# Decoder layer on one core: reordering in out, up and down, and four sums per chunk on VectorE

## What is computed

```python
mix = hybrid_mixer(x, w_in, b_gates, w_sc_conv, mh_gain, w_out)   # gated convolution | mLSTM, then w_out
x = layer_norm(alpha * x + mix, ln1_g, ln1_b)
hid = causal_dwconv(einsum('bsd,df->bsf', x, w_up), w_ffn_conv, b_ffn_conv)
val, gate = hid[..., :5632], hid[..., 5632:]
ff = einsum('bsf,fd->bsd', silu(gate) * val, w_down)
x = layer_norm(alpha * x + ff, ln2_g, ln2_b)
```

## Time and profile before

| | |
|---|---|
| median of 3 runs | 2234.39 us (2232.96 to 2235.47) |
| profiled execution | 2231.34 us, of it span 2229.5 us |
| granted TensorE clock, mean | 0.987 |
| busy in the span | PE 2152.3, PEld 1926.9, DVE 1550.8, ACT 937.4, POOL 233.1 us |
| chain that ended last | PE 82%, DVE 8%, DMA 5%, issue 3%, ACT 2% |

### The profile page before, as it was taken

How to read it: one execution, slowest core, us unless ns; L and a number is a source line. 1 busy time by engine, 2 the same in 40 slices (tenths; PEclk the granted TensorE clock), 3 DMA queues, 4 the chain that set the end, 5 groups by cost and what they waited for, 6 DMA issues and landing times.

```text
span 2229.5 us, 31156 instructions
## 1 busy us (share of the span) xinstructions
PE 2152.3 (97%) x12984; PEld 1926.9 (86%) x12984; DVE 1550.8 (70%) x1612; ACT 937.4 (42%) x1092; POOL 233.1 (10%) x197
## 2 busy tenths in 40 slices
PE   8999999999999998899999999999999999999994
PEld 7888888888877878899999999999999878888873
DVE  3354324432339997777777777777777799999998
ACT  4332222221124445455555455554555544444441
POOL 0000000000011212000000000000000123221220
PEclk9999999999999999999999999999999999999997
DMA  6222222242238414667666766676666788775451
GB/s 233 94 95 87 84 94 82 89 170 94 94 136 212 124 76 142 188 171 190 185 176 169 209 182 168 184 200 170 161 175 180 255 201 233 208 232 149 142 177 76
DMA packets 86249, 350.46 MB, mean 157 GB/s; under 512 B 8172, under 2 KB 19468, under 8 KB 73056
## 3 DMA queue, kind: packets, MB, share of 16 engines
q1 hardware_dynamic: 63616, 263.22, 33.9%
q0 software_dynamic: 22496, 85.30, 19.5%
HBM read 324.36 MB, written 24.12 MB: 156 GB/s over the span
## 4 chain that ended last, share of the span: by engine, by line
PE 82%; DVE 8%; DMA 5%; issue 3%; ACT 2%; SPq 0%; POOL 0%; DVEq 0%; ACTq 0%; POOLq 0%
PE ps L1686 27%; PE ps L1687 27%; PE ps L1688 27%; DMA unit_odd<-w_up 2%; DVE slot_lo L1410 1%; DMA hb<-h_dram 1%; DVE acc L1616 1%; ACT slot_hi L924 1%; DMA oa<-w_out 1%; DVE oslot_lo L1282 1%; DVE slot_lo L1564 1%; DMA raw<-w_mix 1%; DMA unit_even<-w_up 0%; DVE acc L1636 0%; DVE dx L1588 0%
## 5 line engine op out<-in xcount | busy, mean ns | idle before, releaser
L1686 PE MATMUL ps<-xb,slot_hi 128*128 128x256 f32 x2408 | 687.1, 285 | 17.5 <-DVE hid L1432 10.0
L1687 PE MATMUL ps<-xb,slot_hi 128*128 128x256 f32 x2408 | 683.5, 284 | 0.0
L1688 PE MATMUL ps<-xb,slot_lo 128*128 128x256 f32 x2408 | 683.2, 284 | 0.0
L1686 PEld LDWEIGHTS ps<-xb,slot_hi 128*128 128x128 f32 x2408 | 463.9, 193 | 24.4 <-DVE slot_lo L1410 16.4
L1688 PEld LDWEIGHTS ps<-xb,slot_lo 128*128 128x128 f32 x2408 | 464.1, 193 | 0.0
L1687 PEld LDWEIGHTS ps<-xb,slot_hi 128*128 128x128 f32 x2408 | 464.1, 193 | 0.0
L722 ACT ACTIVATE w_hi<-raw 128x2048 fp32r<-128x2048 f32 x56 | 107.3, 1916 | 424.6 <-PE ps L1688 422.0
L1073 DVE TENSOR_TENSOR w_lo<-raw,w_hi 128x2048 fp32r<-128x2048 f32 x55 | 125.8, 2288 | 213.7 <-ACT w_hi L722 213.7
L1410 DVE TENSOR_TENSOR slot_lo<-unit_odd,slot_hi 128x1024 fp32r<-128x1024 f32 x154 | 188.7, 1225 | 99.3 <-ACT slot_hi L924 99.0
L1410 DVE TENSOR_TENSOR slot_lo<-unit_even,slot_hi 128x1024 fp32r<-128x1024 f32 x147 | 180.0, 1224 | 105.8 <-ACT slot_hi L924 105.6
L1686 PE MATMUL ps<-act_hi,w_hi 128*128 128x512 f32 x640 | 249.7, 390 | 0.0
(11 more groups left out here) (224 smaller groups left out, 3585.2 us busy)
## 6 DMA issues: line engine op xcount, KB each, us to landing
raw<-w_mix SPq DMA_DIRECT2D x56, 1024.0 KB, 4.7
unit_odd<-w_up SPq DMA_DIRECT2D x88, 512.0 KB, 6.2
unit_even<-w_up SPq DMA_DIRECT2D x84, 512.0 KB, 6.4
da<-w_down SPq DMA_DIRECT2D x16, 2048.0 KB, 11.4
unit_odd<-w_up POOLq DMA_DIRECT2D x44, 512.0 KB, 9.9
unit_even<-w_up POOLq DMA_DIRECT2D x42, 512.0 KB, 9.9
da<-w_down POOLq DMA_DIRECT2D x20, 1024.0 KB, 9.9
oa<-w_out SPq DMA_DIRECT2D x6, 2048.0 KB, 9.8
```

Source lines behind the costliest of these rows:

```text
L1686: pe.matmul(dst, a[0], b[0], start=first, stop=False, skip_group_check=onto)
L1687: pe.matmul(dst, a[0], b[1], start=False, stop=False, skip_group_check=onto)
L1688: return pe.matmul(dst, a[1], b[0], start=False, stop=last, skip_group_check=onto)
```

## The change

Four things, three of order and one of engine:

1. out: POOL issues the s1 accumulates before the sums; in chunk 0 the sums also wait for four out_lo. SP waits for both s1 accumulates before it loads A12 (and A22 behind it).
2. up, group 1: DVE's `hid_add` stands ahead of `up_lo_part`; SP stores hidden tile 0 after the loads of group 3's weights, not before.
3. down, start: SP loads A12 of chunk 0 after hb21 and the store of hidden tile GROUPS - 1.
4. down: t1 to t4 of each chunk move from POOL to DVE, at fixed slots. POOL keeps the DMAs; in chunk 1 its residual accumulate stands ahead of s3. The semaphores yc_hi and hc_hi become one (tokens_hi), counted on.

```diff
@@ SP, out
             load_out(0, A21, oa21)
+            for i in range(2):
+                sp.wait_ge(s1_added[i], 16)
             load_out(0, A12, oa12)
@@ SP, up
             for m in range(1, GROUPS - 1):
-                store_hidden(m - 1)
+                if m > 1:
+                    store_hidden(m - 1)
                 for b, i in FREED:
...
                     load_unit_block(m + 2, b)
+                if m == 1:
+                    store_hidden(0)
@@ SP, start of down
             load_hidden(0, 3, hb22)
-            sp.wait_ge(up_done, N_UP - NP + 2)
-            load_block(0, A12, da12)
             sp.wait_ge(up_lo, N_UP - NP + 3)
             sp.wait_ge(s4_up, GROUPS)
             load_hidden(0, 2, hb21)
             store_hidden(GROUPS - 1)
+            sp.wait_ge(up_done, N_UP - NP + 2)
+            load_block(0, A12, da12)
@@ POOL, out
-            pool.wait_ge(ym_h, 8)
-            pool.wait_ge(conv_u, 8)
             for c in range(OUT_CHUNKS):
                 y11, y12, y21, y22 = out_blocks(c)
+                for p in (0, 2):
+                    out_s1(c, p)
                 if c:
-                    for p in (0, 2):
-                        out_s1(c, p)
                     pool.wait_ge(yc_lo, NP * c)
+                else:
+                    pool.wait_ge(ym_h, 8)
+                    pool.wait_ge(conv_u, 8)
+                    pool.wait_ge(out_lo, 4)
                 pool.tensor_tensor(ty[:, :, :], y12, y11, ALU.subtract).then_inc(t1_sum, 1)
-                if c == 0:
-                    for p in (0, 2):
-                        out_s1(c, p)
@@ POOL, down (down_t1 to down_t4 removed)
             for c in range(CHUNKS):
                 g = CHUNK_PAIRS[c]
-                down_t1(c, g)
-                down_t2(c, g)
+                if c == 1:
+                    add_residual(0, 1, NP)
                 for p in range(0, g, 2):
                     down_s3(c, p)
-                down_t3(c, g)
-                if c == 1:
-                    add_residual(0, 1, NP)
-                down_t4(c, g)
@@ DVE, up
                 m, i = unit_of(n)
+                add = n and ORDER[(n - 1) % NP] in ("P2", "P7", "P3")
+                if add and m == 1:
+                    hid_add(n - 1)
                 if n + AHEAD < N_UP:
                     up_lo_part(n + AHEAD)
...
-                if n and ORDER[(n - 1) % NP] in ("P2", "P7", "P3"):
+                if add and m > 1:
                     hid_add(n - 1)
@@ DVE, down
+            def down_t4(c):
+                g = CHUNK_PAIRS[c]
+                dve.wait_ge(hb_in[2], 16 * (c + 1))
+                dve.wait_ge(t2_sum, OUT_CHUNKS + c + 1)
+                dve.wait_ge(hc_lo, NP * c + 4)
+                dve.tensor_tensor(hy[:, 0:g, :], hb21[:, 0:g, :], hb11[:, 0:g, :], ALU.subtract).then_inc(t4_sum, 1)
...
                 if s + DOWN_AHEAD < N_DOWN:
                     down_lo_part(s + DOWN_AHEAD)
+                if s == 0:
+                    down_t1(0)
+                if s == 1:
+                    down_t2(0)
+                if i == 6 and c + 1 < CHUNKS and p in (1, 2):
+                    (down_t1 if p == 1 else down_t2)(c + 1)
+                if i == 1 and p == 2:
+                    down_t3(c)
+                if i == 3 and p == 2:
+                    down_t4(c)
                 for what, chunk, pair in sums_after(s):
```

More of the change, by code:

```diff
@@ L257, in build @@
         s2_out, s4_out = sem("s2_out"), sem("s4_out")
-        yc_hi, yc_lo = sem("yc_hi"), sem("yc_lo")
+        tokens_hi, yc_lo = sem("tokens_hi"), sem("yc_lo")
         out_hi, out_lo, out_done = sem("out_hi"), sem("out_lo"), sem("out_done")
@@ L285, in build @@
         t1_sum, t2_sum, t3_sum, t4_sum = sem("t1_sum"), sem("t2_sum"), sem("t3_sum"), sem("t4_sum")
-        hc_hi, hc_lo = sem("hc_hi"), sem("hc_lo")
+        hc_lo = sem("hc_lo")
         down_hi, down_lo, down_done, half_done = sem("down_hi"), sem("down_lo"), sem("down_done"), sem("half_done")
@@ L659, in down_s3 @@
                                accum_op=ALU.add, max_dma_last_dim=4096).then_inc(s3_added[p // 2], 16)
[L661 to L683, removed]
             for p in range(0, CHUNK_PAIRS[0], 2):
@@ L860, in y_split @@
                 act.activation(yc[k % 2][:, 0, :, :], out_src(c, what), ACT.Copy,
-                               scale=-1.0 if what in NEGATED else 1.0).then_inc(yc_hi, 1)
+                               scale=-1.0 if what in NEGATED else 1.0).then_inc(tokens_hi, 1)
             def ln_sqrt(done, first, last):
@@ L1039, in hid_split @@
                 act.activation(hc[k % 2][:, 0, 0:g, :], src[:, 0:g, :], ACT.Copy,
-                               scale=-1.0 if what in NEGATED else 1.0).then_inc(hc_hi, 1)
+                               scale=-1.0 if what in NEGATED else 1.0).then_inc(tokens_hi, 1)
             hid_split(0, 0)
@@ L1287, in y_lo_part @@
                 c, what = k // NP, OUT_ORDER[k % NP]
-                dve.wait_ge(yc_hi, k + 1)
+                dve.wait_ge(tokens_hi, k + 1)
                 hi, lo = yc[k % 2][:, 0, :, :].bitcast(F32), yc[k % 2][:, 1, :, :]
@@ L1569, in hid_lo_part @@
                 src = {"P1": hb11, "P2": hb21, "P6": hb11, "P5": hy, "P7": hb12, "P3": hb22, "P4": hy}[what]
-                dve.wait_ge(hc_hi, k + 1)
+                dve.wait_ge(tokens_hi, OUT_KS + k + 1)
                 if what in NEGATED:
@@ L1594, in down_s4, with down_t1, down_t2, down_t3 @@
                 dve.tensor_tensor(da12[:, p, :], da12[:, p, :], dx[:, p, :], ALU.add).then_inc(s4_down, 1)
+            def down_t1(c):
+                g = CHUNK_PAIRS[c]
+                for b in range(2):
+                    dve.wait_ge(hb_in[b], 16 * (c + 1))
+                dve.tensor_tensor(hy[:, 0:g, :], hb12[:, 0:g, :], hb11[:, 0:g, :], ALU.subtract).then_inc(t1_sum, 1)
+            def down_t2(c):
+                g = CHUNK_PAIRS[c]
+                dve.wait_ge(hb_in[3], 16 * (c + 1))
+                dve.wait_ge(t1_sum, OUT_CHUNKS + c + 1)
+                dve.wait_ge(hc_lo, NP * c + 1)
+                dve.tensor_tensor(hb11[:, 0:g, :], hb22[:, 0:g, :], hy[:, 0:g, :], ALU.subtract).then_inc(t2_sum, 1)
+            def down_t3(c):
+                g = CHUNK_PAIRS[c]
+                dve.wait_ge(t1_sum, OUT_CHUNKS + c + 1)
+                dve.tensor_tensor(hb12[:, 0:g, :], hb22[:, 0:g, :], hb12[:, 0:g, :], ALU.subtract).then_inc(t3_sum, 1)
+            def down_t4(c):
+                g = CHUNK_PAIRS[c]
+                dve.wait_ge(hb_in[2], 16 * (c + 1))
+                dve.wait_ge(t2_sum, OUT_CHUNKS + c + 1)
+                dve.wait_ge(hc_lo, NP * c + 4)
+                dve.tensor_tensor(hy[:, 0:g, :], hb21[:, 0:g, :], hb11[:, 0:g, :], ALU.subtract).then_inc(t4_sum, 1)
             def add_out(k, u):
```

## The result

| | before | after |
|---|---|---|
| median, same chip | 2232.96 us (2231.37 to 2235.47) | 2244.72 us (2243.73 to 2247.04) |
| ratio | | 1.0055, 95% interval 1.0043 to 1.0067 |
| profiled execution | 2231.34 us, span 2229.5 | 2244.8 us, span 2243.0 |
| DVE, POOL busy | 1550.8, 233.1 us | 1539.7, 168.5 us |
| granted TensorE clock, mean | 0.987 | 0.986 |

A forecast was written before the change was run, and what follows sets the result against it. TensorE was taken as the bound, busy 2152.3 of 2229.5 us, VectorE second in out and down. Terms +0.5 - 4.0 - 3.8 - 0.3 + 1.0 + 4.8 = -1.8 us, from median 2234.39 to 2232.6 us; range 2225 to 2242.

The forecast's parts named there:

- Part 1, out: Out: the 7.0 us wait at its start goes but returns three products later as 4.8 us; about +0.5 us.
- Part 2, up: Up: earlier hid sums and unit 3 loads shrink TensorE's 5.0 us wait to 2.2; -4.0 us (-5.5 to -2).
- Part 3, the start of down: Start of down: hb21 lands before da12 and VectorE is held less by POOL's sums; -3.8 us (-5.5 to -1).
- Part 4, the turns: Down's chunk changes: late t4 delays loads; +1.0 us among four-pair chunks, +4.8 at the last turn; -0.3 for VectorE's load.
- rival 1: Whole kernel: the gains stay, s1 of the last turn landing in time; -6.6 to -9.8, about 2226 us; chance 0.31 with its form.
- Rival 2: Down: t4's date also makes turns 0 to 3 late, through s1 or hb22; +8 to +10, about 2241 us; chance 0.26.
- Rival 1's form: Down: VectorE gains by every sum taken off GpSimd, so the 3.6 us of acc waits go too; 0.31 together with rival 1.

The follow-up runs named there:

- the orders alone: The kernel before with the changed orders in out, up and the start of down, the four sums left on POOL: 2225.82 us, ratio 0.9966.
- the sums alone: The kernel before with only the four sums per chunk moved to DVE, out, up and start of down in old order: 2251.30 us, ratio 1.0080.
- A21 first: The changed kernel with SP asking for the next chunk's A21 before it waits for t4 and loads hb11; t4 stays late: 2222.86 us, ratio 0.9952.
- t4 early: The changed kernel with t4 of each chunk five slots earlier on DVE (1796.85 for 1810.97): 2222.74 us, ratio 0.9956.

## Why the prediction was wrong, by its own steps

**Part 1, out (+0.5).** Right. No wait at 666.8, and the old one came back behind: 1.33, 1.38 and 3.99 us instead of 7.00. The long one stood at 692.1, not at 702.6; VectorE was held up earlier than I had drawn it. At the end of out the same matmul ends at 824.47 us in the changed kernel and at 824.48 before, so the net is 0.0.

**Part 2, up (-4.0).** Right, a little small. The wait of 5.03 us at 917.4 became 0.49, because VectorE goes straight on to its sum at 916.10 instead of 918.97. The traces of the changed kernel and of the orders alone both gain 6.4 us from the first copies of up to 927 us and lose 1.2 and 1.1 of it again by the end of up, in part in small waits for hid, so 5.1 and 5.2 stay. Before up, the changed kernel lies 1.7 us behind, though no edit lies between out and up; seven other traces of the same code up to there are 0.6 to 1.5 us behind, so part of this is the scatter of single traces.

**Part 3, the start of down (-3.8).** Right in size, but the attribution was loose. hb21 came ahead of da12, and the wait of 4.8 us is one of 2.94 (the sum written there, -0.6 - 5.4 + 2.3, is -3.7 and not -3.8). What VectorE was spared belongs to the move of the sums: in the kernel with the orders alone, whose sums are on POOL, it is held as before,

```profile
1772.95 3.42 DVE L1595 TENSOR_TENSOR dx<-da,da 128x1024 f32<-128x1024 f32 x1
1776.28 3.41 DVE L1571 TENSOR_TENSOR slot_lo<-da,slot_hi 128x1024 fp32r<-128x1024 f32 x1
...
1781.89 3.91 DVE L1571 TENSOR_TENSOR dslot_lo<-dx,dslot_hi 128x1024 fp32r<-128x1024 f32 x1
```

and the start of down gains 1.7 us by the order alone, 2.9 by the sums alone and by both 3.7 (A21 first), 3.8 (t4 early) and 5.1 (changed kernel, where no restart followed).

**Part 4, the turns: the step that failed.** I had +1.0 at turn 0 to 1, nothing at 1 to 2 and +4.8 at 4 to 5; they cost 10.3, 1.9 and 10.4. With these in place of mine the sum is +0.5 - 4.0 - 3.8 - 0.3 + 22.6 = +15.0; the span shows +13.5.

At turn 4 to 5 the mechanism was right and a term was too small. da21 went out 12 to 13 us later against TensorE's position, as forecast; s1 took 15.6 us where I had allowed 9.7 to 12.8. The step from 9.7 to 12.8 was worth 3 us in my own working, so 15.6 makes it about +9. The rows that I took as bounds were of accumulates with loads spread out beside them. The same trace had a dearer one: of the two s1 accumulates at turn 0 to 1, the one issued at 1823.59 took 18.4 us. And I had written under rival 1 that the loads would now go out in one bundle beside it, but put it into no number.

At turn 0 to 1 I looked for the wrong transfer. I weighed s1 and hb22, whose dates move, and found 1 to 3 us to spare. The late one was hb21, whose date doesn't move against TensorE's position (1833.59 before, 1824.98 with a lead of 8.6 us). Its duration does: 18.6 us before, as this row has it, and 31.8 after.

```profile
hb<-h_dram SPq DMA_DIRECT2D x1, 512.0 KB, 18.6
```

I had followed the dates of issue and carried durations over from the old trace. But from 1840 to 1860 the DMA engines were full already before (1.03 in the earlier trace rows), and in such a stretch a load takes as long as the bytes asked for around it need. Much of the right sum was there to be made: 3 MB (hb11, da21 and hb12) go out 16, 12 and 9 us later against TensorE's position, into a stretch that has no room for them, so the last load in it lands late. How much of the 13 us this sum would have given is said below.

The Trainium skill, DMA: Bandwidth & Descriptors, section Queues, rings and completion order, says that each DMA engine takes turns among the queues that have work. The trace agrees where it can be seen: when less is asked for behind it on POOL's queue, hb21 lands 11 us sooner, some 8 of them for that reason.

**The rivals.** Rival 2 (late loads through t4) came true in kind, with other places and twice its price; it had two or three us per turn in up to four turns, not ten in two. Rival 1's form, a gain by every sum taken off GpSimd, is right in sign once the dates are kept: 2222.74 us with the sums on VectorE and t4 early, 2225.82 with them on POOL, measured on the same chip, and no run of one lies in the range of the other. But this isn't a gain in every chunk. From the fourth product of down to its end the lead over the kernel before stays as it is in both traces (8.7 and 8.6 us, 6.4 and 6.3), and the 3.6 us of acc waits that were to go are 3.4. VectorE is held less there (the mean of `slot_lo<-da` is 1218 ns instead of 1384), but TensorE doesn't wait for that; the gain stands at the start of down, as far as the traces show it. And it was outweighed seven times over by what one of the sums released.

**Left open.** Parts 2 and 3 were not run one by one; their split rests on the traces. The wait at turn 1 to 2 (1.66 us) was not followed to its transfer. Why hb21's landing moves by more than the DMA time that is missing (13.1 us for 25 x 0.30 = 7.5) is not settled. Counted in bytes it is nearer: 262 less 148 GB/s over 25 us are 2.9 MB, and at the 294 GB/s of the full stretch these take 9.7 us, an estimate. Accumulates falling together with it is one reason that would do, argued only.

## What to carry to other kernels

When an operation changes its engine, ask first what its end releases, and put it in the new order by that, not by a slot that is free: moved by 14 us, t4 turned a loss of 12 us into a gain of some 10. Where the DMA engines are full, don't reckon with the durations of the old trace; count the bytes that must be through by a date, and look at the idle DMA time ahead of that stretch, because it can't be made up. The transfer that suffers may be one whose issue the change doesn't touch.

## What the runs showed that I had not expected

- A 512 KB load asked for at the same moment takes 18.8 to 36.0 us, depending on when 2 to 3 MB before it were asked for; with two 1 MB accumulates behind it made small it takes 20.9 us instead of 31.8, of which some 3 us come of its own loads going out sooner (an estimate).
- The cost of a late sum grows faster than its delay: t4 at 1796.9, 1805.7, 1811.0 and two slots on gives 2222.7, 2230.0, 2244.7 and 2265.3 us, since more turns run out of slack.
- 2 MB of weights earlier by 10 us are as good as everything earlier. The two orders of loads reach the same time within 0.1 us.
